# Neighbourhood attention: when the bias arrives, and how the last norm is made

## The reference, cut to what matters

```python
def neighbourhood_attention(h, w_qkv, q_norm, k_norm, rpb, w_out):
    qkv = (h @ w_qkv).reshape(bsz, rows, GRID_W, 3, NA_HEADS, NA_HEAD_DIM)
    q = rmsnorm_2(qkv[:, :, :, 0], q_norm) * (NA_HEAD_DIM ** -0.5)   # norm over the 64 channels of a head
    k = rmsnorm_2(qkv[:, :, :, 1], k_norm)
    v = qkv[:, :, :, 2]
    ...
    s = einsum(q_blk, k_blk) + bias      # bias from rpb by relative row and column, -inf outside the window
    pr = softmax(s); o = einsum(pr, v_blk)
    return out @ w_out
```

## Time and profile before

| | us |
|---|---|
| median of 3 runs (lowest, highest) | 2922.69 (2921.74, 2930.5) |
| the profiled execution, whole | 2931.41 |
| its span, first to last instruction | 2929.7 |
| mean granted TensorE clock in the span | 0.975 |

### The profile page before, as it was taken

How to read it: one execution, slowest core, us unless ns; L and a number is a source line. 1 busy time by engine, 2 the same in 40 slices (tenths; PEclk the granted TensorE clock), 3 DMA queues, 4 the chain that set the end, 5 groups by cost and what they waited for, 6 DMA issues and landing times.

```text
span 2929.7 us, 39664 instructions
## 1 busy us (share of the span) xinstructions
PE 2813.6 (96%) x15582; PEld 2440.7 (83%) x15583; DVE 1948.7 (67%) x2308; ACT 1403.2 (48%) x1568; POOL 277.0 (9%) x248
## 2 busy tenths in 40 slices
PE   6989999989999999999998999999999999998999
PEld 5868988877888888887877888888888988996888
DVE  5585453647888888887454763785477577585775
ACT  2223422216767776775433552343555455435554
POOL 0004851400000000000001000002100010020000
PEclk8969999999999999999999999999999999999999
DMA  8855564267999999997552563433356456572553
GB/s 262 273 175 162 178 211 131 89 230 256 336 346 366 335 341 356 357 339 278 185 203 87 192 199 119 140 115 115 116 188 221 140 167 200 165 205 69 182 184 112
DMA packets 504828, 609.70 MB, mean 208 GB/s; under 512 B 50201, under 2 KB 371836, under 8 KB 504700
## 3 DMA queue, kind: packets, MB, share of 16 engines
q1 hardware_dynamic: 502224, 606.82, 62.3%
q10 hardware_dynamic: 2476, 1.06, 0.1%
HBM read 605.75 MB, written 1.05 MB: 207 GB/s over the span
## 4 chain that ended last, share of the span: by engine, by line
PE 80%; DVE 7%; DMA 4%; POOL 3%; issue 3%; ACT 3%; SPq 0%; DVEq 0%; ACTq 0%; POOLq 0%
PE bank L1450 13%; PE bank L2038 7%; PE bank L1454 7%; PE bank L1442 7%; PE bank L1267 4%; PE bank L1884 4%; PE bank L1888 4%; PE bank L1897 4%; PE bank L1797 3%; PE bank L1319 3%; PE bank L1946 2%; DMA ring<-in_o_exp_down 2%; PE bank L1937 2%; PE bank L1938 2%; PE bank L1802 1%
## 5 line engine op out<-in xcount | busy, mean ns | idle before, releaser
L3287 DVE TENSOR_TENSOR ring_r<-ring,store_area_r 128x2048 fp32r<-128x2048 f32 (+1 forms) x344 | 809.1, 2380 | 200.4 <-ACT store_area_r L2449 197.4
L2449 ACT ACTIVATE store_area_r<-ring 128x2048 fp32r<-128x2048 f32 (+1 forms) x344 | 670.7, 1974 | 229.0 <-PE bank L1454 57.2
L1450 PE MATMUL bank<-hT_sq_r,store_area_r 128*128 128x512 f32 x1376 | 347.2, 394 | 0.6 <-DVE ring_r L3287 0.6
L1450 PEld LDWEIGHTS bank<-hT_sq_r,store_area_r 128*128 128x128 f32 x1376 | 249.0, 190 | 45.7 <-DVE ring_r L3287 0.9
L2038 PE MATMUL bank<-hT,ring 128*128 128x256 f32 x1024 | 229.9, 380 | 0.0
L3743 DVE TENSOR_TENSOR ring_r<-ring,store_area_r 128x3072 fp32r<-128x3072 f32 x64 | 195.0, 3087 | 49.2 <-ACT store_area_r L2882 49.1
L2038 PEld LDWEIGHTS bank<-hT,ring 128*128 128x128 f32 x1024 | 190.8, 190 | 27.0 <-issue 3.1
L1454 PEld LDWEIGHTS bank<-hT_sq_r,ring_r 128*128 128x128 f32 x1376 | 188.0, 191 | 13.5
L2882 ACT ACTIVATE store_area_r<-ring 128x3072 fp32r<-128x3072 f32 x64 | 163.5, 2561 | 73.7 <-DMA ring<-in_o_exp_down 58.0
L1454 PE MATMUL bank<-hT_sq_r,ring_r 128*128 128x256 f32 x1376 | 192.0, 282 | 0.0
L1193 POOL TENSOR_TENSOR silu_g<-silu_g 128x768 f32<-128x768 f32 (+2 forms) x14 | 29.9, 2136 | 1708.4 <-ACT silu_g L2461 1337.9
(11 more groups left out here) (560 smaller groups left out, 4800.8 us busy)
## 6 DMA issues: line engine op xcount, KB each, us to landing
ring<-in_o_exp_gate SPq DMA_DIRECT2D x88, 1024.0 KB, 7.1
ring<-in_o_exp_up SPq DMA_DIRECT2D x88, 1024.0 KB, 7.3
ring<-in_ffn_w_gu SPq DMA_DIRECT2D x88, 1024.0 KB, 6.9
ring<-in_o_exp_down SPq DMA_DIRECT2D x32, 1536.0 KB, 8.8
ring<-in_ffn_w_down SPq DMA_DIRECT2D x32, 1408.0 KB, 8.7
ring<-in_o_exp_down SPq DMA_DIRECT2D x32, 1280.0 KB, 11.6
ring<-in_ssd_w_in SPq DMA_DIRECT2D x32, 1024.0 KB, 7.1
ring<-in_e_mod_mix_w SPq DMA_DIRECT2D x12, 1024.0 KB, 8.7
```

The costliest lines, as they stand in the source:

```text
L1450: mm(bank[:, :], w_hi(k), x_both(k), start=(start and k == blocks[0]), stop=False)
L2449: activation(dst, slot(u, s, kk), ACT.Copy).then_inc(w_high, 1)
L3287: nc.vector.tensor_tensor(slot(u, s, kk, rounded=True), slot(u, s, kk), as_f(high), ALU.subtract).then_inc(w_low, 1)
```

## The change

It has two parts. The bias loads are issued after the weights of unit 3 and before those of units 4 and 5, and not after unit 5. And the norm of n = 3 (k of heads 8 to 15) is made by rows: the four sums go to four strips of 32 partitions of one bank (16 rows for either of its two heads), ACT takes the root of 128x256 and not of 128x1024, DVE inverts 128x256, and TensorE spreads the factor of each head over its 64 partitions with a matrix `na_spread`, which ACT builds from the identity; these four matmuls (`factors_spread`) stand in unit 5, before its last quarter. DVE then multiplies k by the factors in two halves, straight from banks 6 and 7. As `scores(1)` writes these banks, the wait for `qk_ready` 4 moves from `scores(4)` to `scores(1)`.

```diff
@@ SP
-                    columns(stage, w3("na_w_qkv_2", 0))
+                    w = w3("na_w_qkv_2", 0)
+                    columns(stage, w, 4)
                     for half, low in ((0, -2), (1, -3)):
                         for i in range(6):
...
                             sp.dma_start(na_bias[64 * half:64 * half + 64, :, i, :], src).then_inc(rpb_in, 16)
+                    for c in (4, 5):
+                        u = Unit(base[stage] + c)
+                        freed(u)
+                        for s in range(2):
+                            load(u, s, w[:, :, 2 * COLS * c + s * COLS:2 * COLS * c + (s + 1) * COLS])
@@ TensorE, unit(c)
+                            if (c, s, t) == (5, 1, 1):
+                                factors_spread()
@@ TensorE, head_sums(n)
                     for j in range(4):
+                        if n == 3:
+                            i = mm(banks[6][32 * j:32 * j + 32, 0:T], halves[:, 48:80], act[:, 4 + j, :], start=True, stop=True)
+                            continue
...
+                def factors_spread():
+                    pe.wait_ge(na_factor_ready, 2)
+                    for j in range(4):
+                        i = mm(banks[6 + j // 2][:, (j % 2) * T:(j % 2 + 1) * T], na_spread[:, j * P:(j + 1) * P], rs[:, 0:T],
+                               start=True, stop=True)
+                        if j % 2:
+                            i.then_inc(factor_cols, 1)
@@ TensorE, scores(s)
-                    if s == 4:
+                    if s == 1:
                         pe.wait_ge(qk_ready, 4)
@@ ACT, roots(n)
+                    if n == 3:
+                        activation(na_spread.rearrange("p (h d) -> p h d", d=64),
+                                   ident[:, :].rearrange("p (h n) -> p h n", n=16)[:, :, 0:1].to_broadcast([P, 8, 64]), ACT.Copy)
+                        activation(rs[:, 0:T], banks[6][:, 0:T], ACT.Sqrt, bias=small[:, 0:1], scale=1.0 / 64).then_inc(qk_std, 1)
+                        return
@@ DVE, c == 3
                     ve.wait_ge(qk_std, c + 1)
+                    t = flat2((na_q, na_k)[c // 2][:, 4 * (c % 2):4 * (c % 2) + 4, :])
+                    if c == 3:
+                        nc.vector.reciprocal(rs[:, 0:T], rs[:, 0:T]).then_inc(na_factor_ready, 1)
+                        ve.wait_ge(evac, base["na_in"] + c + 1)
+                        for j in range(2):
+                            ve.wait_ge(factor_cols, j + 2)
+                            half = t[:, 2 * T * j:2 * T * (j + 1)]
+                            ins = nc.vector.scalar_tensor_tensor(out=half, in0=half, scalar=vc[:, 1, KN_ROW:KN_ROW + 1],
+                                                                 in1=banks[6 + j][:, :], op0=ALU.mult, op1=ALU.mult)
+                        ins.then_inc(qk_ready, 1)
+                        continue
```

More of the change, by code:

```diff
@@ L579, in program @@
     na_cols = small[:, 64:66]
+    na_spread = rs[:, T:3 * T]
     def ffn_square(k, n=1):
@@ L4042, in na @@
                     ve.wait_ge(evac, base["na_in"] + c + 1)
-                    t = flat2((na_q, na_k)[c // 2][:, 4 * (c % 2):4 * (c % 2) + 4, :])
                     gain = qn_col[:, :] if c < 2 else vc[:, 1, KN_ROW:KN_ROW + 1]
```

## The result

| | before | changed |
|---|---|---|
| median of 20 runs, us | 2927.11 | 2933.97 |
| lowest, highest | 2921.74, 2931.68 | 2927.63, 2938.21 |
| profiled execution: whole, span | 2931.41, 2929.7 | 2933.76, 2932.0 |
| mean granted clock | 0.975 | 0.974 |

The ratio changed to before is 1.0021, 95% interval 1.0015 to 1.0027: 6.1 us slower (4.4 to 7.9). The forecast was no change that a measurement can tell, leaning slower by 3.3 us. The direction held, and the interval leaves 1 out, so that 20 runs of each do tell a change smaller than the 8.8 us that the prediction took for the limit. 2933.97 lies above the range's 2931.5. Of the 8.0 us between 2926.0 and the result, 4.4 is the base (the median of three runs shown before was 2922.69, that of 20 is 2927.11) and 3.6 the size of the change (6.9 between the medians, 3.3 forecast).

The account below looks back on a forecast made before the run. DVE was taken to bound the stretch to the first maxima, TensorE close behind; maxima 1.8 us later plus 1.5 for the clock gave +3.3, 2934.7 profiled, 2926.0 without a profile; range 2919.5 to 2931.5.

Parts of the forecast that it names:

- The bound and its change: From unit 3's end to the first maxima DVE bounds, TensorE and ACT close behind; the later rhythm of 16 heads stays unchanged.
- Masks between DVE's instructions: At unit 4's low parts POOL's masks take turns with DVE, so unit 3's copy out starts 3.8 us later.
- When the masks start: POOL's masks, shifted 27.4 us with the whole pattern of bias loads, start at 2593.8 instead of 2621.2.
- Weights behind the biases: Unit 4's weights, queued behind the bias loads, land at 2596.5 and 2599.4; alone, this delay is hidden in DVE's pause.
- Rival (c): Unit 4's weights land late behind the bias loads, delaying DVE and TensorE: +12.6 us, 2935; chance 0.05.
- The wait at the spread: Before unit 5's last quarter TensorE waits 2.9 us for DVE's inverse of 128x256.
- the term left at 0 of 0 to 1.5: TensorE's four sums to four strips of one bank could overlap, gaining between 0 and 1.5 us; taken as 0.
- The clock: After TensorE's 2.9 us pause, 3.3 us at half clock on the path to the scores cost 1.5 us.
- rival (b): The spread's wait costs its 1.8 us, but the clock does not fall in time: 2924.5; chance 0.15.
- The sum: First maxima at 2638.8 against 2637.0, 1.8 us later, plus 1.5 for the clock: +3.3 us, 2926.0 without a profile.
- Runs without a profile sat 8.7 lower in the median: Distance from profiled execution to unprofiled median, used to turn the profiled 2934.7 into the forecast 2926.0.
- 3.1 less: DVE's product of n = 2, no longer meeting POOL's masks, falls from 4.42 to 1.28 us.

Follow-up runs that it names:

- tied masks: Changed kernel with POOL's masks 0 and 1 started with unit 3's copy out, 2 and 3 with unit 5's low parts; ratio to before 1.0007.
- two later profiles: The changed kernel, unedited, profiled and timed twice more against the kernel before; ratios 1.0015 and 1.0016.
- Norm only: Changed kernel with the old order of the bias loads, so only the norm differs from the kernel before; ratio to before 1.0008.
- bias only: Kernel before with the new, sooner order of the bias loads and the norm as before; ratio to before 1.0013.
- both mends: Changed kernel with POOL's masks started beside DVE's inverses and the spread's four matmuls moved behind unit 5; ratios to before 0.9991 and 0.9982.
- filler: Changed kernel with seven matmuls, their result overwritten, ahead of the spread's wait to keep TensorE busy; ratio to before 1.0023.
- late spread: Changed kernel with the four matmuls of the spread moved from before unit 5's last quarter to behind unit 5; ratio to before 1.0003.
- norm only with the late spread: Changed kernel with the old order of the bias loads and the spread's four matmuls moved behind unit 5; ratio to before 0.9995.

## Why the prediction was right and wrong

**The bound and its change.** Right. DVE set the first maxima before, TensorE does now, and the rest of the attention kept its length (32.18 and 32.20 us from the maxima to the next stage in the first pair of profiles).

**Masks between DVE's instructions.** Right as a mechanism: they start 33 us sooner, the low parts of unit 4 are held one by one (4.88 and 5.57, forecast 4.5 and 5.7), one mask takes 5.53 (forecast 5.8), and tied masks remove all but 0.4 us at each of two products. The page "SBUF — State Buffer" of the Trainium skill, in "Who interferes with whom", has both the instructions that block and those that do not; the copies with one SBUF input, 1.27 beside a mask, agree. The prediction left out an exception of that page: it frees an instruction with at most one SBUF input only outside the two-port modes, and counts `tensor_scalar` among those that can enter them. The `TENSOR_SCALAR` of 128x2 that took 0.98 us instead of 0.17 beside a mask is in line with that; it played no part in the changed kernel, whose masks end long before the maxima. What the page does not say, who is next when both wait, came out as the engine that had waited longer each time here: POOL behind a DVE instruction, DVE behind a mask.

**When the masks start.** Wrong by 4 us: 2588.1 and not 2593.8 - 1.4 (the stage itself began 1.4 sooner in this execution). I shifted the whole pattern of the loads by 27.4 us, but it did not stay the same: the twelve issues took 20.03 us and not 21.28, and the masks began 4.3 us behind their end (2588.1 against 2583.86) and not 6.9 (2621.2 against 2614.29). By this the masks also met the product of n = 0, a third hold that I had not forecast. The delay of unit 3's copy out, 3.6 us (2607.11 - 2603.26, less the 0.2 of before), is near my 3.8 by luck: DVE was held by masks 0, 2 and 3, where I had masks 1 and 2.

**Weights behind the biases.** No later than forecast, and no cost: ACT went on to unit 4's first slot at 2594.89 without a wait, where the forecast, shifted by the same 1.4, had it land at 2595.1. Rival (c) is out.

**The wait at the spread.** Right: 2.70 us against 2.9. TensorE's sums were the term left at 0 of 0 to 1.5; they gained 1.0, which brought TensorE to the wait sooner, and so was worth nothing. The wait at the start of unit 5 was 1.3 to 2.0, forecast 0.4. In the two later profiles the wait at the spread was 1.2 and 1.3, because slow clock in unit 5 had made TensorE come later.

**The clock.** Right in the first profile: half the clock after the pause, 1.6 to 1.7 us, forecast 1.5. In the two later profiles it fell behind the first pause of unit 5 instead and cost nothing at the end, which is how rival (b) had it: one profile of three went by the forecast and two by that rival.

**The sum.** For the changed kernel the prediction's first maxima, with the clock, stand 35.6 us behind the sums (2638.8 + 1.5 - 2604.7); measured were 36.1, 35.1 and 35.2. The steps that failed are on the side of the kernel before.

The first is the base, and it alone took the result out of the range. "Runs without a profile sat 8.7 lower in the median" set one profiled execution against the median of three runs, and the sum used it as a fixed distance. Over 20 runs the difference was 4.3 (2931.41 against 2927.11), and in the thirteen other profiles the profiled execution lay between 4.2 us below and 5.3 us above the median of its own runs, 0.3 below in the mean. With 2927.11 as the base the same working gives 2930.4 and a range that ends near 2936, with 2933.97 in it. With a scatter of 8.8 us in three runs on record, the 3.8 us left for scatter at the upper end was too little.

The second is the term "3.1 less" for the product of n = 2, and with it D 32.3 as the kernel before. Over three profiles that hold was 3.1, 3.0 and 1.0 us, 2.4 in the mean. D is 31.6 before and 35.5 changed in the mean, 3.9 apart, and single pairs lie between 2.7 and 5.8; with the rest of the stage it is 64.0 and 67.7. So +3.3 was some 0.5 us too small by the profiles.

The measured 6.1 (4.4 to 7.9) is above that, the two later ratios (4.4 and 4.7 us, each about 3 either way) are near it. Whether 1 to 2 us more lie outside the stage is left open. The profiles show none behind it: from the start of the next stage to the end of the span all fourteen have 259.0 to 260.6 us, the kernel before 260.5 to 260.6, the changed one 259.0 to 260.5. Ahead of it they scatter by more than what is looked for (sums of n = 2 at 2599.8 to 2607.6 us before, 2601.4 to 2603.3 changed). Norm only and bias only came out 2.4 and 2.5 us above what their profiles say, both mends 0.9 and 3.6 below, and the kernel before against itself scatters by up to 2.3.

## What to carry to other kernels

A wait that is put into the stream of the bounding engine costs by what is queued behind it: put the dependent work behind the last piece that does not need it, not ahead. Work of POOL that is moved out of one collision with DVE can land in the next; look at every DVE instruction with two SBUF inputs in the new place, or tie the POOL work to an instruction of DVE that is long and was not held beside it, here the inverse of 128x1024, 6.54 us with and without a mask. And a collision that hangs on a DMA's landing had a different price in each execution here, so that one profile is one draw of it. The same goes for the base: the median of three runs was 4.4 us off that of 20, more than the change that was forecast.

## What the runs showed of the hardware

- Four matmuls whose results go to four strips of 32 partitions of one bank (128\*32) had a row of 0.64 us for 8 records, against 1.89 for the same sums at 128\*128, and where nothing held it the next work started 1.0 us sooner (0.57 behind the start of the sums with tied masks, 1.54 before).
- DVE and POOL took strict turns in every hold of this stage; the one case ahead of the prediction where three DVE instructions ran through the earlier trace rows, though POOL's row starts 0.15 us ahead of the first of them, did not come again.
- Beside a mask the inverses with one SBUF input kept their 6.54 us and the copies out of PSUM their 1.27, but a `TENSOR_SCALAR` of 128x2 with one SBUF input was held to the mask's end, 0.98 us instead of 0.17.
- A pause of TensorE of 1.85 to 2.70 us was followed by half the clock for some 3.4 us in all three profiles of the changed kernel, and so was one of 2.61 in the filler's. Pauses of 1.2 to 1.3 were not, and neither was one of 2.34 with the late spread. In the kernels with both mends the clock fell 9 to 10 us into the attention with no pause longer than about 1 us ahead of it in the attention, only many short ones; in norm only with the late spread it fell about 5 us in, 2 us behind a pause of 1.85, and stayed down for some 7 us.
